# First block of a two-model forward pass: dilated groups 1 and 2 with rows sorted by remainder mod 4, units of four heads, stick-breaking units moved to the middle

## The reference, cut to what matters

```python
A_GROUPS = ((128, 1), (512, 4), (2048, 16))      # (window, dilation), 4 heads each
def dilated_attention(q, k, v, table_a):
    for gi, (window, d) in enumerate(A_GROUPS):
        # rows t, t+d, t+2d, ... form d sequences; banded attention in each
        dist, mask = band_layout(lp // BLK, window // d)
        bias = band_bias(table_a[:, gi], dist * d)[:, None]
        num, m, l = banded_attention(to_sub(q[:, :, gi], d, lp)[:, :, None], ...)
    c = jnp.exp(ms - jnp.max(ms, axis=2, keepdims=True))     # over the three groups
    out = jnp.sum(c[..., None] * nums, axis=2) / jnp.sum(c * ls, axis=2)[..., None]
def sliding_window_gqa(...):       # branch B: 8 query heads, 2 key heads, window 128, a sink per head
def stick_breaking_attention(...): # branch C: 4 heads, all earlier keys, a suffix sum of log_sigmoid
merged = g0 * (o_a @ w_br_a) + g1 * (o_b @ w_br_b) + g2 * (o_c @ w_br_c)
```

## Time and profile before

| | |
|---|---|
| median of 3 runs | 3360.75 us |
| the profiled execution | 3353.29 us, span 3351.5 us |
| TensorE busy | 3249.6 us (97%) |
| VectorE, ScalarE busy | 1698.9 us (51%), 1405.0 us (42%) |
| slots 8 to 41 of the mixer | 67.00 to 409.75 us |

### The profile page before, as it was taken

The page is one execution under the profiler, slowest core; times in us unless marked ns, Lnnn a source line. Parts: engine busy times, 40 slices in busy tenths (PEclk is TensorE's granted clock), DMA queues, the critical chain, the costliest instruction groups (busy, mean ns, idle before and its releaser), DMA issues.

```text
span 3351.5 us, 56510 instructions
## 1 busy us (share of the span) xinstructions
PE 3249.6 (97%) x22192; PEld 2973.1 (89%) x22192; DVE 1698.9 (51%) x2451; ACT 1405.0 (42%) x2001; POOL 36.4 (1%) x53
## 2 busy tenths in 40 slices
PE   8999998999999899999999999999999999999997
PEld 6787686787887699999899999999999989999997
DVE  3444454774575544435667544344444556654434
ACT  3334433663343355424542554335542454245532
POOL 0000000000000000000000000000000000000000
PEclk9999999999999999999999999999999999999998
DMA  4111133222222122232111222222222211122222
GB/s 167 55 56 51 57 107 102 75 96 92 94 94 94 61 90 94 88 100 82 57 57 64 88 88 93 95 94 88 91 91 95 87 51 58 63 88 88 90 98 94
DMA packets 78277, 282.65 MB, mean 84 GB/s; under 512 B 8814, under 2 KB 8814, under 8 KB 78048
## 3 DMA queue, kind: packets, MB, share of 16 engines
q1 hardware_dynamic: 74880, 270.57, 24.3%
q0 software_dynamic: 2000, 8.53, 0.7%
q10 hardware_dynamic: 1296, 2.14, 0.2%
HBM read 279.06 MB, written 2.15 MB: 84 GB/s over the span
## 4 chain that ended last, share of the span: by engine, by line
issue 70%; PE 27%; DVE 1%; ACT 1%; POOL 1%; POOLq 0%; DVEq 0%; ACTq 0%; DMA 0%; SPq 0%
PE ps L1465 12%; PE ps L1526 8%; PE ps L1540 1%; PE ps L1975 1%; PE ps L1566 1%; PE ps L1601 1%; PE ps L1589 1%; PE ps L1572 0%; PE ps L1609 0%; PE ps L1633 0%; PE ps L1629 0%; PE ps L1580 0%; POOL d_rstd L490 0%; POOL r_rstd L490 0%; POOLq L489 0%
## 5 line engine op out<-in xcount | busy, mean ns | idle before, releaser
L511 ACT ACTIVATE w_hi<-w_raw 128x1024 fp32r<-128x1024 f32 x512 | 542.5, 1060 | 1193.3 <-PE ps L1465 1014.1
L895 DVE TENSOR_TENSOR w_lo<-w_raw,w_hi 128x1024 fp32r<-128x1024 f32 x512 | 625.7, 1222 | 566.8 <-ACT w_hi L511 566.8
L1465 PE MATMUL ps<-h_hi,w_hi 128*128 128x264 f32 (+1 forms) x3376 | 793.4, 303 | 31.3 <-DVE h_lo L906 29.4
L1465 PE MATMUL ps<-h_hi,w_lo 128*128 128x264 f32 (+1 forms) x3376 | 789.4, 303 | 0.0
L1465 PE MATMUL ps<-h_lo,w_hi 128*128 128x264 f32 (+1 forms) x3376 | 788.9, 302 | 0.0
L1465 PEld LDWEIGHTS ps<-h_hi,w_hi 128*128 128x128 f32 x3376 | 544.4, 189 | 69.2 <-issue 19.2
L1465 PEld LDWEIGHTS ps<-h_lo,w_hi 128*128 128x128 f32 x3376 | 540.2, 188 | 24.5 <-issue 2.2
L1465 PEld LDWEIGHTS ps<-h_hi,w_lo 128*128 128x128 f32 x3376 | 541.7, 189 | 22.6
L1465 PE MATMUL ps<-f_hi,w_hi 128*128 128x264 f32 (+1 forms) x1664 | 387.5, 302 | 2.0 <-DVE f_lo L1123 2.0
L1465 PE MATMUL ps<-f_lo,w_hi 128*128 128x264 f32 (+1 forms) x1664 | 386.9, 301 | 0.0
L1465 PE MATMUL ps<-f_hi,w_lo 128*128 128x264 f32 (+1 forms) x1664 | 386.4, 301 | 0.0
(11 more groups left out here) (290 smaller groups left out, 3852.1 us busy)
## 6 DMA issues: line engine op xcount, KB each, us to landing
w_raw<-in_stream SPq DMA_DIRECT2D x512, 512.0 KB, 3.3
xT<-in_x ACTq DMA_DIRECT2D x8, 256.0 KB, 9.8
bias_a<-bias_scratch POOLq DMA_DIRECT2D x2, 1024.0 KB, 9.6
xT<-in_x POOLq DMA_DIRECT2D x1, 2048.0 KB, 9.8
out<-tmp SPq DMA_DIRECT2D x8, 256.0 KB, 2.1
const<-in_const POOLq DMA_DIRECT2D x1, 1636.0 KB, 9.2
bias_b<-bias_scratch POOLq DMA_DIRECT2D x1, 1024.0 KB, 14.4
params<-in_params POOLq DMA_DIRECT2D x1, 535.5 KB, 7.6
```

The costliest lines, as they stand in the source:

```text
L511: nc.scalar.activation(w_hi[:, s, :], w_raw[:, s, :], ACT.Copy).then_inc(hi_done, 1)
L895: V.tensor_tensor(w_lo[:, s, :], w_raw[:, s, :], w_hi[:, s, :].bitcast(F32), ALU.subtract).then_inc(lo_done, 1)
L1465: last = T.matmul(out[:, p, :], w[:, s, j * P:(j + 1) * P], x[:, k, c0:c1], start=start and j == 0 and r == 0, stop=stop and j == len(ks) ...
```

## The change

1. Tiles 2 to 5 of A's queries, keys and values (groups 1 and 2) are written by the eviction with their columns sorted by remainder mod 4 (`RESIDUE_TILES`, a stride of four elements in the source and in `rstd`).
2. Units of A hold four heads of group 0 alone (4 units, 28 blocks). New units D hold four heads, groups 1 and 2, one remainder: one key block for each group (4 units, 32 blocks).
3. The four heads of a unit of A, D or B now alternate between the two halves of the partitions (`heads1`), and the products of the two halves go to different banks of PSUM. B's units are regrouped for this.
4. The output, negated maximum and sum of D are kept by remainder (`od_r`), brought back to row order by 16 matmuls with 32-row pieces of a permutation (`permute`, slot 30), and joined with group 0 (`joint_*`, slots 31 to 33). The permutation is made at the start on VectorE.
5. C's units start in slots 12, 15, 18 and 21 and end in slot 25; D stands in slots 25 to 29, B in 31 to 40. `c_weights` comes after `split_hi` in its slot.
6. The bias is loaded by 10 DMAs in place of 4; its table has 896 columns in place of 640.
7. The branch products take C's tiles first; the last three of the eight tiles (6, 4, 5) are split in slot 41.

```diff
-REV_TILES = list(range(AQ, AQ + 6)) + list(range(BQ, BQ + 4))
+REV_TILES = [AQ, AQ + 1] + list(range(BQ, BQ + 4))
+RESIDUE_TILES = [t + i for t in (AQ, AK, AV) for i in range(2, 6)]
...
-        units1 = ([("A", h, b) for h0 in (0, 2) for b in range(NBLK) for h in (h0, h0 + 1)]
-                  + [("B", g, b) for b in range(NBLK) for g in range(2)]
-                  + [("C", h, 0) for h in range(C_HEADS)])
+        units1 = ([("A", 0, b) for b in range(NBLK)] + [("D", 0, r) for r in range(4)]
+                  + [("B", u, b) for u in range(2) for b in range(NBLK)])
...
-        first_slots = list(range(9, 17)) + list(range(18, 26)) + list(range(26, 34))
-        slot_p1 = {p: n for n, p in enumerate(first_slots)}
-        slot_cv = {36: 0, 37: 1, 39: 2, 40: 3}
+        slot_p1 = {p: n for n, p in enumerate(list(range(8, 12)) + list(range(25, 29)) + list(range(31, 39)))}
+        slot_c = {12 + 3 * c: c for c in range(C_HEADS)}
+        slot_cum = {p + 2: c for p, c in slot_c.items()}
+        slot_rest = {p + 3: c for p, c in slot_c.items()}
+        slot_cv = {p + 4: c for p, c in slot_c.items()}
+        SLOT_PERM, SLOT_JOINT = 30, 32
...
-        slot_o = {28: 0, 29: 1, 36: 2, 37: 3, 38: 4, 39: 5, 40: 6, 41: 7}
+        slot_o = {37: [0], 38: [1], 39: [2], 40: [3, 7], 41: [6, 4, 5]}
...
+        def heads1():
+
+            return [(2 * a + c, 2 * c + a, a, c) for c in range(2) for a in range(2)]
...
                 split_hi(*following(p // 2, p % 2))
+                if p in slot_rest:
+                    c_weights(slot_rest[p])
+                if p in slot_c:
+                    c_exps(slot_c[p])
...
-                for br, ks in enumerate((range(0, 2), range(2, 6), range(6, 8))):
-                    pe.wait_ge(ol_done, ks[-1] + 1)
+                for br, ks in ((2, range(6, 8)), (0, range(0, 2)), (1, range(2, 6))):
+                    pe.wait_ge(ol_done, max(order_o.index(k) for k in ks) + 1)
...
+                for _, _, a, c in heads1():
+                    out, lo = ps[:, 3 * s + a, 2 * P * c:2 * P * c + nk], HD * a
+                    if kind == "D":
+                        for g in range(2):
+                            last = T.matmul(out[:, P * g:P * (g + 1)], qkv[lo:lo + HD, AQ + 2 + 2 * g + c, P * b:P * (b + 1)],
+                                            qkv[lo:lo + HD, AK + 2 + 2 * g + c, P * b:P * (b + 1)], start=True, stop=True)
...
+                for r in range(4):
+                    for b in range(NBLK):
+                        rows = slice(P - 32 * (b + 1), P - 32 * b)
+                        last = T.matmul(ps[:, b, 0:A_HEADS * (HD + 2)], perm[rows, r, :],
+                                        od_r[rows, r, :, :].rearrange("p h e -> p (h e)"), start=r == 0, stop=r == 3)
```

More of the change, by code:

```diff
@@ L365, in rev, with t_batches @@
             return slice(SEQ - P * (b + 1), SEQ - P * b)
[L367 to L376, removed]
+        def t_batches(n):
+            nb, w = blocks1(n), width1(n)
+            blocks = [(pos * w + i * P, pos * nb + i) for pos in range(4) for i in range(nb)]
             return [blocks[i:i + 4] for i in range(0, len(blocks), 4)]
-        batch_at = [sum(len(t_batches(x)) for x in units1[:n]) for n in range(N1)]
+        batch_at = [sum(len(t_batches(i)) for i in range(n)) for n in range(N1)]
         def t_bank(s, j):
@@ L553, in exps @@
             def exps(n):
-                kind, h, b = units1[n]
-                s = n % 2
+                s, w = n % 2, width1(n)
                 act.wait_ge(l_done, n + 1)
[L557 to L575, removed]
+                for pos, k, _, _ in heads1():
+                    row = logit[:, s, pos * w:(pos + 1) * w]
+                    last = nc.scalar.activation(row, row, ACT.Exp, bias=neg_max1(n)[:, k:k + 1], accum_out=row_sum1(n, k))
+                last.then_inc(p_done, 1)
             def turned(n):
                 s = n % 2
-                for j, blocks in enumerate(t_batches(units1[n])):
+                for j, blocks in enumerate(t_batches(n)):
                     act.wait_ge(t_done, batch_at[n] + j + 1)
@@ new lines, in logits @@
+                bias = {"A": bias_a[:, :, 2 * P - nk:], "D": bias_d[:, :, :], "B": bias_b[:, u, :, 2 * P - nk:]}[kind]
+                V.scalar_tensor_tensor(rows[:, :, 0:nk], src, SCALE, bias, ALU.mult, ALU.add)
+                pairs = logit[:, s, 0:4 * w].rearrange("p (a c n) -> p a c n", c=2, n=w)
+                if kind == "B":
+                    V.tensor_copy(pairs[:, :, :, nk], sinks.rearrange("p (a j) -> p a j", a=2)[:, :, 2 * u:2 * u + 2])
+                dve.drain()
+                V.tensor_reduce(by_pair(neg_max1(n)), pairs, AX.X, ALU.max, negate=True).then_inc(l_done, 1)
@@ new lines, in c_logits @@
+            def c_logits(c):
+                s = c % 2
+                if c == 0:
+                    dve.wait_ge(const1_in, 16)
+                dve.wait_ge(cs_done, c + 1)
+                for kb in range(NBLK):
+                    bk, col, nq, place = c_place(kb)
+                    last = V.scalar_tensor_tensor(logit[:, s, place:place + nq], ps[:, 3 * s + bk, col:col + nq],
+                                                  SCALE, cmask[:, 0:nq], ALU.mult, ALU.add)
+                last.then_inc(cl_done, 1)
@@ new lines, in c_products @@
+            def c_products(p, c):
+                s, lo = c % 2, HD * (c % 2)
+                set_free(p, 3 + (c > 0), c - 1)
+                pe.wait_ge(px1_free, ready1(CQ + c // 2))
+                for kb in range(NBLK):
+                    bk, col, nq, _ = c_place(kb)
+                    last = T.matmul(ps[:, 3 * s + bk, col:col + nq], qkv[lo:lo + HD, CK + c // 2, kb * P:(kb + 1) * P],
+                                    qkv[lo:lo + HD, CQ + c // 2, kb * P:SEQ], start=True, stop=True)
+                last.then_inc(cs_done, 1)
@@ new lines, in values @@
+                for pos, k, a, c in heads1():
+                    lo = HD * a
+                    for i in range(nb):
+                        tv, kb = (AV + 2 + 2 * i + c, b) if kind == "D" else (AV + c if kind == "A" else BV, b + 1 - nb + i)
+                        last = T.matmul(ps[:, 3 * s, k * HD:(k + 1) * HD], probT[:, s, pos * nb + i, :],
+                                        qkv[:, tv, kb * P + lo:kb * P + lo + HD], start=i == 0, stop=i == nb - 1)
+                last.then_inc(o_done, 1)
```

406 lines of the change are left out of this document (226 added, 180 removed).

## The result

| | before | changed |
|---|---|---|
| median of 4 runs each | 3360.05 us (3357.5 to 3364.59) | 3310.82 us (3308.64 to 3313.92) |
| profiled execution | 3353.3 us, span 3351.5 | 3308.64 us, span 3306.8 |
| first branch product | 409.75 us | 367.86 us |
| end of the stage that follows it | 523.4 us | 482.1 us |

The ratio is 0.9853, with an interval of 0.9836 to 0.987: 49 us faster. I had forecast 3328 with a range of 3316 to 3342. A second measurement of the same kernel gave 0.9877 (0.9856 to 0.9898), 3315.56 against 3354.79, 39 us. The two traces differ by 41.9 us at the first branch product and by 41.3 us at the end of that stage (the other branch products and the gates between them), so by the traces some 41 us are the change's own. What lies between this and the two measurements is told under experiments 9 and 10.

What follows compares the result with a forecast made beforehand. TensorE, busy 97% of the span, was taken as the bound. Work terms -63.0 + 13.9 + 18.4 - 4.6 + 5.0 = -30.3 and waits and clock -2.6 gave -32.9: 3360.75 to 3328 us, range 3316 to 3342.

Steps and rivals of the forecast that it cites:

- waits of C: TensorE waits 0.95 us for C's weights behind split, table load and exponential, four times: +3.8 us.
- wait at the end: TensorE waits 3.2 us for tile 6's lower part ahead of the first branch product.
- its clock stretch: One half-clock stretch behind the wait ahead of the first branch product: +1.8 us.
- a fixed part remains ... 0.20 a pair: Products on two halves overlap in columns; a pair costs 0.20 us fixed, in all 0.41 at 128 columns, 0.62 at 256.
- 7.5 under the median of the runs, which I carry over as it is: Profiled execution of before, 3353.3 us, lay 7.5 under the runs' median; same distance assumed after: 3320.4 profiled, 3328 median.
- The old branch A's 63 us: The 16 units of branch A of before go, with their products, values and turns: -63.0 us.
- All three old waits in C: TensorE's three waits among C's units at the end go, 7.8 us, with 3.6 us of clock: -11.4 us.
- The cover for VectorE's joining steps and evictions: VectorE's joining steps, some 5 us over three slots, and strided evictions of 12 tiles stay hidden: costed at nothing.
- Rival 1: The halves don't overlap for these product forms and the permutation: 11 us less gain, 3339 us; chance 0.12.
- Rival 2: C in the middle stalls as it did at the end, 15.2 us in place of 3.8: 3339 us; chance 0.12.
- Rival 3: More gained: four row groups at once (-2.5), no end clock stretch (-1.8), fewer halves behind foreign matmuls: 3323 us; chance 0.23.
- Rival 4: The strided eviction becomes the bound, pushing TensorE from 2.1 us beyond its length; 3365 us at 5.2 beyond; chance 0.02.

Runs made afterwards that it cites:

- experiments 9 and 10: The kernel before and the changed kernel, each run again unchanged: 3358.5 us and 3315.56 us.
- narrow: Changed kernel with half the columns in D's products (64 for 128) and in the permutation's matmuls (132 for 264): 3307.97 us in one run.
- weights_first: Changed kernel with C's table load and exponentials put ahead of the weight split in the same slot on ScalarE: 3307.62 us.
- both_waits: Changed kernel with c_weights ahead of the weight split, tile splits spread over slots 36 to 41, and branch products waiting tile by tile: 3301.39 us.
- before_again: The kernel before run once more, unchanged, for a second profile: 3358.5 us.
- lower_only: Changed kernel with all four heads of a unit of A, D and B read from the lower half of the partitions, same banks: 3321.59 us in one run.
- perm_rows: Changed kernel with the permutation's two loops swapped, four matmuls of one row group and bank following each other: 3317.6 us in one run.

## Why the prediction was wrong in size

Its own steps, in its order, against the distances between starts in the changed trace:

| step | predicted | measured |
|---|---|---|
| products of A | 4.5 | 3.84 (0.64, 1.07, 1.06, 1.07) |
| turns and values of A | 9.4 | 9.4 |
| products of D | 7.6 | 4.76 (4 x 1.19) |
| turns and values of D | 10.8 | 10.5 |
| products of B | 9.1 | 7.66 |
| permutation | 5.0 | 2.00 |
| waits of C | 3.8 | 4.0 |
| wait at the end | 3.2 | 3.2 |
| its clock stretch | 1.8 | 1.7 (23.49 less 21.78) |
| first branch product starts | 375 | 367.86 |

**The step that failed** is "a fixed part remains ... 0.20 a pair", with what I built on it. I had split into a fixed part for each pair and 0.21 for each 128 columns, the same for a pair of 16 columns as for one of 128. `narrow` shows that this is no straight line: 4 pairs of 64 columns take 1.09 and 4 of 128 take 1.19, so a pair costs some 0.3 whatever it has up to 128 columns. Then the 0.64 of the earlier trace rows is twice 0.32, and a pair of 128 is 0.32 where I took 0.41, one of 256 is 0.53 where I took 0.62. That is 0.7 us in A and 1.4 in B. For D I took the middle between pairs and one half alone; the order lower, lower, upper, upper overlaps fully (1.19 in place of 1.9), 2.8 us with the cheaper pair. For the permutation I took pairs, the nearest row, though the program goes round four row groups: 3.0 us. Together 7.9 us, and less the unforeseen 0.7 of waits for L1072 this is the 7.2 us by which the branch product came earlier than I had said.

The rest is my last step, "7.5 under the median of the runs, which I carry over as it is". For the profiled execution my sum gave 3320.4. Less 7.9 and with the 0.7 it would have been 3313.2; it was 3308.6. Of the 44.7 us between the two profiled executions 41.3 are gained by 482.1 us. The other 3.4 lie behind, where the second trace of the changed kernel, with 2831.4 us from there to its end in place of 2824.7, has nothing of them (before 2828.1). The 4.6 more between the medians are their distance to the profiled executions, 6.8 us before and 2.2 after. So the failed term is 7 us, and with it mended the forecast would have been 3321, inside the range and what the second measurement says (39 us under its own before, in part by luck: its runs of the changed kernel had the lower clock).

The other 10 us of the miss are four pieces: 1.2 in the stage, which became 0.6 us longer where I had put 1.8, since its eight branch products took 0.14 us less each (a cause is not shown); the 3.4 and the 4.6 above; and 0.7 by which the median of before fell when its fourth run came in. Of the 3.4 the clock explains some 2 (the spans lose 3.8 us less to it, 1.8 of that in the mixer). For the 4.6 the clocks of before's runs in the first measurement aren't on record, so their cause stays open. My range had nothing for any of this; experiments 9 and 10 ask for some 5 us at each end.

**What held.** The old branch A's 63 us are gone and turns and values came out within 0.3 us. All three old waits in C went, and the clock stretches behind them. The four waits of 1.0 us came where and as long as worked out (split, load, exponential: 3.7 between 136.26 and 139.96), as did the 3.2 us at the first branch product; `weights_first` and `both_waits` show both by their absence. The clock stretch behind the 3.2 came too, in both traces of the changed kernel, but `narrow` has the wait without it and `before_again` has its own wait of 3.2 without one: the 1.8 for "one" was a guess that came true, not a rule. The cover for VectorE's joining steps and evictions held, except 0.7 us.

**The rivals.** Rival 1 (no overlap) is `lower_only` by its own edit, and costs 12.1 us of products against the changed kernel, more than the 8.2 I gave it for A, B and D, because the pairs are cheaper than I took them; the trace decides against it. Rival 2 (C stalls as before) fell: no wait in slots 14 to 25 is longer than 1.01. Rival 3 named the right side, four row groups at once, at -2.5, and I gave it 0.23; it lacked the cheaper pair and D, and its term for no clock stretch at the end did not come. Rival 4 (evictions) fell: 0.40 us beyond today's length where 2.1 was the first that anyone could feel.

**The two rules.** For the permutation the Trainium skill ("TensorE: Matmul & The Clock Gate", Part 3) gives 3.07 for four row tiles, by which I had estimated 2.6 us. The trace shows 2.00, and only in the order that goes round the four row groups and banks; with one row group and bank at a time it is 4.98. Against my bound of 8.0 (an estimate from 0.5 a matmul, which no run has for 32 rows) that is a factor of 4, against `perm_rows` one of 2.5, and the page's figure lies between. For the eviction the Trainium skill ("Vector Engine (DVE) Microarchitecture Reference", The SBUF access granule) gave an estimated 1.36 us. The trace shows 1.09: 0.8 ns a column on top of 0.69 us. The rule has the right sign and is too high here.

## What to carry to other kernels

Products that fill only half or a quarter of TensorE's rows should be issued so that neighbours lie on different rows and in different banks: pairs of 64-row products took 0.32 in place of 0.54 us at 128 columns and 0.53 in place of 0.96 at 256, four 32-row pieces in turn 0.5 in place of 1.25 with one row group and bank at a time, and the order inside the loop is all that it takes. Before a price is read as "fixed part plus slope" from groups of mixed sizes, ask whether the small member sits on a floor. And of a gain read from two traces, compare the stretch that was changed, since the clock's stretches elsewhere moved the whole by 7 us between two executions of one kernel.

## What the runs showed beside

- How far TensorE overlaps ahead depends on the order: lower, lower, upper, upper is as good as alternation (1.19), four and four is not (1.64 between 1.19 and 1.98).
- A pair of 64-row products has a floor near 0.3 us; 64 columns in place of 128 save 0.1 us in four pairs.
- An eviction with sorted rows takes 1.09 us in place of 0.69, reversed or not.
- Four waits of 1.0 us, each behind a stretch of full work, left the clock at 2.4 GHz (mean 1.00). The wait of 3.2 us was followed by a stretch at 1.2 GHz in both traces of the changed kernel and not in `narrow`; in the two traces of before the wait of 3.2 had one behind it once. The same wait in the same place does not settle the clock.
- A later branch product takes 5.46 us where before took 5.60, at the same clock and of the same form. Only their order among the branches and the waits between them differ; it was not tried apart and stays open.
- Not tried either: both halves writing one bank, and the permutation's row groups in turn with one bank at a time.
